# The attention's input product of a two-layer trunk in 24 steps of seven products, with the stored sums of tokens and W_out formed by GpSimd

## What is computed

```python
def _gla_mixer(x, w_in, w_gk, b_gk, norm_w, w_out):
    h = (x @ w_in).astype(jnp.float32)          # (2048, 1024) @ (1024, 3088)
    q, k, v, g, lr = jnp.split(h, [512, 1024, 2048, 3072], axis=-1)
    gk = jax.nn.log_sigmoid(lr @ w_gk + b_gk) / 16
    ...                                          # per head: cumulative sums of gk over chunks of 64,
    qe, ke, kd = q * exp(bcum), k * exp(-bcum), k * exp(b_last - bcum)
    ...                                          # attention of qe, ke, kd, v; norm; times silu(g)
    return o.astype(x.dtype) @ w_out
```

## Time and profile before

| | |
|---|---|
| median of 3 runs | 2005.15 us (2003.45 to 2006.34) |
| profiled execution, own time | 2001.48 us |
| its span, first to last instruction | 1999.6 us |
| TensorE busy | 1914.5 us (96%) |
| VectorE, ScalarE, GpSimd busy | 1161.7, 701.3, 431.5 us |

### The profile page before, as it was taken

The page is one execution under the profiler, slowest core; times in us unless marked ns, Lnnn a source line. Parts: engine busy times, 40 slices in busy tenths (PEclk is TensorE's granted clock), DMA queues, the critical chain, the costliest instruction groups (busy, mean ns, idle before and its releaser), DMA issues.

```text
span 1999.6 us, 24456 instructions
## 1 busy us (share of the span) xinstructions
PE 1914.5 (96%) x8974; PEld 1588.5 (79%) x8974; DVE 1161.7 (58%) x1539; ACT 701.3 (35%) x1065; POOL 431.5 (22%) x268
## 2 busy tenths in 40 slices
PE   8999999999999989999949999999999999999997
PEld 7778887888888778888738888887888886787786
DVE  4330102332415277787675688868678657546998
ACT  4441213131313243343354444344434335224331
POOL 0005200000000000000043666423334343322430
PEclk9999999999999999999979999999999999999999
DMA  8766530334233464455322444333322225647342
GB/s 254 221 202 239 178 103 17 108 87 118 79 101 87 159 242 164 172 187 170 136 96 74 153 141 152 135 104 137 129 88 73 94 74 193 249 170 272 129 177 95
DMA packets 229912, 287.74 MB, mean 144 GB/s; under 512 B 17216, under 2 KB 170176, under 8 KB 227904
## 3 DMA queue, kind: packets, MB, share of 16 engines
q1 hardware_dynamic: 225216, 278.20, 42.0%
q10 hardware_dynamic: 4608, 8.39, 1.1%
HBM read 186.93 MB, written 99.61 MB: 143 GB/s over the span
## 4 chain that ended last, share of the span: by engine, by line
PE 41%; DVE 4%; issue 4%; ACT 1%; POOL 0%; DVEq 0%; POOLq 0%; ACTq 0%
PE banks L165 13%; PE banks L166 13%; PE banks L167 13%; DVE m_w_lo L1922 1%; DVE m_x_lo L1936 1%; ACT m_x_hi L1728 0%; DVE m_x_lo L1914 0%; PE banks L1621 0%; PE banks L1668 0%; DVE m_stats L2025 0%; DVE m_x_lo L1896 0%; DVE m_res L2019 0%; DVE m_res L2035 0%; POOL m_s L1859 0%; DVE m_win_b L1968 0%
## 5 line engine op out<-in xcount | busy, mean ns | idle before, releaser
L165 PE MATMUL banks<-m_x_hi,m_w_hi 128*128 128x512 f32 x1320 | 517.6, 392 | 9.4 <-DVE m_res L2019 3.5
L166 PE MATMUL banks<-m_x_lo,m_w_hi 128*128 128x512 f32 x1320 | 515.3, 390 | 0.0
L167 PE MATMUL banks<-m_x_hi,m_w_lo 128*128 128x512 f32 x1320 | 515.0, 390 | 0.0
L165 PEld LDWEIGHTS banks<-m_x_hi,m_w_hi 128*128 128x128 f32 x1320 | 248.7, 188 | 63.7 <-DVE m_w_lo L1922 10.0
L166 PEld LDWEIGHTS banks<-m_x_lo,m_w_hi 128*128 128x128 f32 x1320 | 248.8, 188 | 52.0 <-issue 0.7
L167 PEld LDWEIGHTS banks<-m_x_hi,m_w_lo 128*128 128x128 f32 x1320 | 248.7, 188 | 52.0
L1854 POOL TENSOR_TENSOR m_s<-pair_raw 128x512 f32<-128x512 f32 x24 | 47.3, 1969 | 891.6 <-POOLq L947 757.5
L165 PE MATMUL banks<-x_hi,h_w_hi 128*128 128x512 f32 x512 | 199.9, 390 | 0.8 <-DVE h_g_out L833 0.8
L166 PE MATMUL banks<-x_lo,h_w_hi 128*128 128x512 f32 x512 | 199.3, 389 | 0.0
L167 PE MATMUL banks<-x_hi,h_w_lo 128*128 128x512 f32 x512 | 199.3, 389 | 0.0
L1716 ACT ACTIVATE m_w_hi<-m_s 128x512 fp32r<-128x512 f32 x184 | 115.5, 629 | 202.7 <-PE banks L167 179.2
(11 more groups left out here) (220 smaller groups left out, 3117.7 us busy)
## 6 DMA issues: line engine op xcount, KB each, us to landing
p_in<-in_pool_w_in SPq DMA_DIRECT2D x32, 256.0 KB, 4.9
p_rows<-in_x SPq DMA_DIRECT2D x16, 512.0 KB, 5.2
w_fused<-p_out SPq DMA_DIRECT2D x32, 256.0 KB, 3.9
h_out_rows<-in_pool_w_out SPq DMA_DIRECT2D x16, 512.0 KB, 6.7
v_tiles<-v_out ACTq DMA_DIRECT2D x32, 256.0 KB, 2.1
w_terms<-h_out_terms SPq DMA_DIRECT2D x8, 1024.0 KB, 5.6
h_raw<-in_gla_w_in SPq DMA_DIRECT2D x16, 512.0 KB, 4.2
g_tiles<-h_g_out SPq DMA_DIRECT2D x32, 256.0 KB, 2.3
```

The lines of the kernel that those rows point to most:

```text
L165: nc.tensor.matmul(out, a_hi, b_hi, start=first, stop=False, skip_group_check=True)
L166: nc.tensor.matmul(out, a_hi, b_lo, start=False, stop=False, skip_group_check=True)
L167: return nc.tensor.matmul(out, a_lo, b_hi, start=False, stop=last, skip_group_check=True)
```

## The change

The input product is cut into 24 steps (`STEPS`), eight for the values (`V_STEPS`, i = 0 to 7: one pair of token tiles by all 1024 value columns) and twice eight for gates, queries and keys (one unit of 2x128 columns by one half of 1024 tokens). A step is seven block products of four `split_product`s each, in the order `ORDER`, position `n` of a step; the names 1 to 7 are block products. One operand (`w_hi[j]`, `w_lo[j]`, 128x512 each) is new in each step: ScalarE rounds it (`hi_part`), VectorE makes the rest (`lo_part`), one step ahead. The other operand (`b_hi[j]`, `b_lo[j]`, 128x2048 each, seven of them) stays for eight steps: first W_v, then either half of x.

- `prepare` no longer splits x. It stores the turned tiles to device memory (`x_in`, 16 stores of 512 KB), loads the four blocks of W_v (1 MB each, SP at n = 10, 12, 14, 16), has GpSimd form their sums (16 operations), and has ScalarE and VectorE split the seven blocks at n = 18, 20, ... 30, ScalarE behind a wait for all 16 sums.
- Each step's pair of blocks (two transfers of 512 KB into `raws[i % 2]`) is loaded by SP; GpSimd forms its four sums (`weight_sums`). In the value steps GpSimd also forms one round of W_out's sums (`out_terms`) and four sums of the tokens (`x_terms`), both into the one buffer `terms`, each stored by SP (1 MB) before the next writes it. The token sums go to `x_in`, from which the seven blocks of a half of x are loaded at steps 7 and 15 (`load_x`, 1 MB each).
- The gate's first factor, cumulative sums, queries, keys and gates are the same arithmetic over halves of 1024 tokens, placed by tables (`Q_AT`, `K1_AT`, ...) in step and position. `load_qkv` stands behind the last stores of the stage. `w_fused` is stored in rows, and read by columns in the last stage.

```diff
 def prepare(nc, p, a):
+    V_LOADS_AT = {10: 1, 12: 7, 14: 3, 16: 2}
+    V_PARTS_AT = {n: j for n, j in zip(range(18, 32, 2), ORDER)}
...
+                def store_x(t):
+                    sp.wait_ge(x_copied, t + 1)
...
                 b11, b12, b22, b21 = (p.b_raw[j] for j in V_LOADS)
+                for j in V_LOADS:
+                    pool.wait_ge(b_loaded[j], DMA)
+                for k in range(HALF_K):
+                    nc.gpsimd.tensor_tensor(p.b_raw[5][:, k, :], b12[:, k, :], b11[:, k, :], ALU.subtract)
...
                     if n >= 1:
                         copy_out(n - 1)
+                    if n in V_PARTS_AT:
+                        act.wait_ge(b_summed, 4 * HALF_K)
+                        j = V_PARTS_AT[n]
+                        nc.scalar.activation(p.b_hi[j][:], p.b_raw[j][:], ACT.Copy).then_inc(b_hi_done, 1)
...
 def project(nc, p, a):
+            def product(i, n):
+                j = ORDER[n]
+                pe.wait_ge(w_lo_done, PRODUCTS * i + n + 1)
+                free(i, j)
+                for k in range(HALF_K):
+                    last = split_product(nc, shaped(i, bank(i, j)), w_hi[j][:, k, :], w_lo[j][:, k, :],
+                                         moving(i, x_hi[j], k), moving(i, x_lo[j], k), opens and k == 0, k == HALF_K - 1)
...
+            (SP, position n of value step i)
+                        if n == 3:
+                            store_out_terms(i)
+                            if i + 1 < 2 * HALF_K:
+                                load_out_rows(i + 1)
+                        elif n == 5:
+                            sp.wait_ge(x_summed, 4 * (i + 1))
+                            sp.wait_ge(w_lo_done, PRODUCTS * (i + 1))
+                            load_pair(i + 2)
+                            store_v(i, 0)
+                            store_x_terms(i)
...
+            (ACT, position n of step i)
+                    elif n == 0:
+                        seed(i)
+                    elif n == 2:
+                        copy_u2(i)
+                    elif n == 3:
+                        copy_p5(i)
+                    for turn in turning(TURN_HI, i, n):
+                        turn_hi(*turn)
+                    if n >= 0:
+                        hi_part(i + 1, n)
...
+            weight_sums(0)
+            for i in range(STEPS):
+                if i + 1 < STEPS:
+                    weight_sums(i + 1)
+                if i < V_STEPS:
+                    for part in range(2):
+                        out_terms(i, part)
+                    for part in range(2):
+                        x_terms(i, part)
```

More of the change, by code:

```diff
@@ L182, in prepare @@
     t_lo = [p.place(f"p_t_lo{s}", [P, GT, P], F32R) for s in range(2)]
-    out = [p.place(f"p_out{s}", [P, GW]) for s in range(2)]
-    rows = [p.place(f"p_rows{s}", [P, D]) for s in range(ROWS)]
+    assert p.at <= SBUF_END
     with ExitStack():
@@ L459, in project @@
[L459 to L470 removed]
+    chunk_end = p.place("h_chunk_end", [P, HALF_CHUNKS])
@@ new lines, in project, with kind, unit, step_of @@
+    w_src = a["gla_w_in"][0].rearrange("(k p) c -> p k c", p=P)
+    N1, N2 = slice(0, BLK), slice(BLK, HALF)
+    MAIN, ALT = 0, 1
+    def kind(i):
+        return "v" if i < V_STEPS else UNITS[i % EPOCH][0]
+    def unit(i):
+        return (i // EPOCH - 1) * HEADS + UNITS[i % EPOCH][1]
+    def step_of(name, m):
+        return (m // HEADS + 1) * EPOCH + STEP_OF[name, m % HEADS]
+    def due(table, i, n):
+        return [(i - r) // EPOCH * HEADS - HEADS + h for h, (r, at) in table.items()
+                if at == n and (i - r) % EPOCH == 0 and 1 <= (i - r) // EPOCH <= 2]
@@ L472, in _, with gates, gate_stores, turns_to @@
+    def gates(m):
+        return g_alt if m % HEADS == 0 else g_main
+    def gate_stores(m, which):
+        return sum((o % HEADS == 0) == (which == ALT) for o in range(m)) * 4 * DMA
+    def turns_to(e, n):
+        return PRODUCTS * (e - 1) + n + 1
+    gk_ps = p.ps[:, 6:8, :].rearrange("p b t -> p (b t)")
+    CHAINED = 5
+    with nc.Block() as block:
         @block.sync
         def _(sp):
-            def load(h, j):
-                sp.dma_start(raw[j % 2][:], w_src[:, :, ds(w_cols(h, j), P)]).then_inc(loaded[j % 2], DMA)
@@ new lines, in gate_rows, with turn_keys @@
+            def gate_rows(m):
+                pe.wait_ge(gk_lo, m + 1)
+                pe.wait_ge(rank_ready, 2 * (m // HEADS + 1))
+                pe.wait_ge(kn_copied, 2 * m)
+                for n in range(2):
+                    nc.tensor.matmul(p.ps[:, 6 + n, :], w_gk[:], rank[:, n * BLK:(n + 1) * BLK], start=True, stop=True
+                                     ).then_inc(gk_mm, 1)
+            def turn_keys(m):
+                pe.wait_ge(k_done, 2 * m + 2)
+                for n in range(2):
+                    for c in range(HALF_K):
+                        t = n * HALF_K + c
+                        last = nc.tensor.transpose(p.ps[:, 6 + n, c * P:(c + 1) * P], sums[:, t * P:(t + 1) * P], p.ident[:])
+                    last.then_inc(turned, 1)
@@ L859, in attend_and_norm @@
+            norm_of(2 * HEADS - 1)
+    for s in held:
+        nc.gpsimd.sem_clear(s)
+        nc.release_semaphore(s)
 def attend_and_norm(nc, p, a):
@@ L960, in load_w @@
                 sp.dma_start(raw[kt % RAW][:], w_src[:, kt, :]).then_inc(raw_loaded[kt % RAW], DMA)
[L962 to L963 removed]
+            for s, n in enumerate((6 * 4, 2 * 4)):
+                sp.wait_ge(p.g_stored[s], n * DMA)
             for kt in range(RAW):
```

1073 lines of the change are left out of this document (665 added, 408 removed).

## The result

The changed kernel takes 2112.2 us (median of four runs, 2110.9 to 2113.9) beside 2004.9 for the kernel before: 1.0545 times as long, 95% interval 1.0531 to 1.0558. It is slower, as forecast, but by 107 us and not by 53.

The account below looks back on a forecast made before the run. TensorE set the pace before; in the value steps GpSimd's chain would. Second stage +21 (61.7 us saving included), first +21, hand-over +11: +53 on 2001.5 gives 2054.5, median 2058 us; range 2022 to 2090.

Parts of the forecast that it names:

- The closed chain: Value steps: GpSimd's sums and their transfers follow without overlap, 28.7 us per round, bounds 25.3 and 32, against TensorE's 19.04.
- product 7 as the place of TensorE's wait: Value steps: TensorE waits once per step at product 7 for `copy_u2`, about 9 us.
- The end of step 8: Second stage: step 8's last product ends near S+253, after the last block of x lands and is split.
- The saved 61.7 us: TensorE's work: 272 fewer matmuls save 61.7 us if nothing else moves.
- The chain costs 81.6 us: Value steps: nine steps end near S+253, where TensorE's pace alone takes 171.4 us; the chain adds 81.6.
- S+30: Value steps: the first token sums end 30 us after S, the second stage's first matmul.
- For stalls I add 8: Second stage after the value steps: VectorE's load, fullest in step 15, stalls TensorE 8 us, bounds 0 and 35.
- The rival of VectorE as the bound: Last 16 steps: VectorE sets the pace, 2 us more in every step, +30, total 2088 us; chance 0.12.
- +21; bounds 10 and 32: First stage: tile 19 waits for W_v's sums, +17, and six other blocks' splits add +4; +21 us.
- T+13.5: Hand-over: third stage starts 13.5 us behind the last matmul T, after copies, stores, issues and landing; +11, bounds 6 and 15.
- Third and last stage at nothing: Third and last stage: no change in length, 0 us in the forecast's sum.
- Contention (2072): Value steps, rival: every pair sum takes 2.0 us, round 30.7 us, +14, total 2072 us; chance 0.15.

Follow-up runs that it names:

- two ways of breaking it: Against the changed kernel: token sums first with W_out's sums formed in place in their own rows, 2032.1 us; or W_out's sums left out, 2029.7 us.
- short pair sums: The changed kernel with GpSimd's pair sums of steps 10 to 23 cut to one column; 2097.4 us, 1.0465 times before.
- W_v loaded earlier: The changed kernel with W_v's four blocks loaded at tiles 2, 4, 6, 8 of the first stage; 2101.1 us, 1.0497 times before.
- all together: The changed kernel with two buffers, third stage's first loads ahead, W_v at tiles 4, 7, 10, 12 and its rest later; 2008.3 us, 1.0031 times before.

## Why the prediction was right and wrong

**Right: direction and mechanisms.** The closed chain (the changed kernel's timeline, and two ways of breaking it, each worth 80 us), product 7 as the place of TensorE's wait, the wait for W_v's sums near tile 19, the landing behind the hand-over: each stands in the profile. The end of step 8 was right by its length alone (24.0 us behind the token sums for 22): the path named was the last block of x, and it was pair 9, ahead of the fifth block's rest in VectorE's stream. The saved 61.7 us of TensorE's work are there too, by the count: the rest of the second stage after the value steps needs 285.6 + 21.8 + 8 = 315.4 us and has 347.2, the value steps need 171.4 and have 269.3, and 616.5 is the sum.

**Wrong: the sizes.** On its own time the profiled execution was forecast at 2054.5 us and took 2111.0. The 56.5 us between are these steps of it:

- *"The chain costs 81.6 us"*: it costs 269.3 - 171.4 = 97.9, 16.3 more. The first token sums begin at 192.16 and end 2.0 us later than S+30. Then come seven rounds, to 400.93, of 29.8 us for 28.7: +7.9. Loads and stores were sized well (6.45 for 6.6, 5.66 for 5.8), and so were the pair sums (6.3 for 6.1); the term that failed is W_out's sums, taken at their undisturbed 5.1 us, which measured 6.4. The token sums of step 7 run beside VectorE's rests of the blocks of x and took 9.7 us instead of 5.1 (last section): +4.5. From there to the end of step 8 is 24.0 us for 22, by another path than the one named.
- *"For stalls I add 8"*: 31.8, 23.8 more, the largest miss and the step that failed most. The prediction took VectorE's load for step 15, let steps of which the sum fits pass for free, and put the lower clock behind a wait at nothing here. Of the 31.8, 21.4 are twelve waits of TensorE, most of them for VectorE's and ScalarE's sums, gates and copies (434.5 to 782 us):

```profile
PE banks L824 <- DVE h_sums L1235: 8.6, 5, 3.7
PE banks L173 <- DVE h_g_main L1131: 5.5, 3, 2.3
PE banks L173 <- ACT h_c L914: 5.3, 2, 2.7
```

  The rest is mostly clock. Around five of the waits, of 1.8 to 3.7 us, the granted clock is 0.50 for 3.4 us each, as here behind the wait of 2.65 us at 479.82 (columns as in the table of stages):

```profile
479.80:482.80 3.00, 2.98 (x7) 2.42 (x8) 2.57 (x5) 0.91 (x2) 0.00 (x0) 0.50 0.08 23
```

  By these figures some 17 us are run at half the pace, an estimated 8 us lost. The short pair sums show 10 of the 32 to be GpSimd's. That the other 22 come from the places of sums, gates and splits in VectorE's and ScalarE's streams was only read, not tried. The rival of VectorE as the bound would have made this term 38 (my 8 and its 30), nearer to 31.8 than 8; in its form, an even 2 us in every step, it is not what the profile shows.
- *"+21; bounds 10 and 32"* for the first stage: +30.0, 9 more, inside the bounds. GpSimd's first sum was taken at 76 and ran at 80.5, which puts tile 19 at +21.5 for +17: 4.5 of it. Behind tile 19 come +8.5 for +4: the six short waits are 6.0 us and not 4, and behind the wait of 14.9 us the clock is 0.50, so that the next twelve matmuls start 0.43 us apart and not 0.23, 2.4 us in all. ScalarE also reached its wait for the sums at 90.5 and not at 83.1, held by a store of `w_fused`; here the sums hid that, in *W_v loaded earlier* it comes out. TensorE's waits for `p_in` are 12.3 us for 8.2 before; the new one (4.8 us) lies ahead of tile 19 while the sums are awaited, and costs nothing further.
- *"T+13.5"* for the hand-over: the third stage begins 17.0 us behind the end of the last product, 17.4 behind its start, from which the forecast counts: 3.9 more. The first store of g is at T+6.4. Its four issues take 2.5 us, the five loads of the first tile 3.1 (priced at 2), and from the last of these issues to TensorE's start it is 5.5 (landing priced at 3 to 4).
- *Third and last stage at nothing*: +3.7. In the profiles of the changed kernel and the nine others these stages, the same in all but one of them, take 1307.3 to 1311.2 us, so up to 4 us of spread is in any single profile. All ten are above the one profile of before (1306.8), so that `w_fused` is now read by columns may have a part in it; this was not tried.

The range ended at 2090 because its ends came from one deviation at a time. Contention (2072) came true in part, though in W_out's sums and not in the pair's, where it was forecast; so did the VectorE case (2088) in size, and the first stage and the hand-over lie near their upper bounds; those summed would have been 2054.5 + 14 + 30 + 11 + 4, beyond 2110.

## What to carry to other kernels

Before moving work to an idle engine, write its round with the transfers that it waits for as a closed chain, and compare that chain, not the engine's busy time, with the pace of the engine that sets the end: one shared buffer between two stores, with the order around it, cost 80 us here, while the same 164 us of GpSimd's work, in a better order and with a buffer for each kind of sum, fitted beside TensorE's. When a cheaper product also moves operand preparation ahead of a stage and stores behind it, the boundaries between stages are part of the price (22 us in the best version, more than the 19 us that the stage gained). Mis-sized terms of one cause (one engine's contention, one fuller queue) go the same way, so a range must add them. A stretch whose sums of work fit still waits where its streams cross, and a longer wait can bring a stretch at the lower clock with it.

## What the hardware showed that was not expected

GpSimd and VectorE slow each other in both directions. VectorE's 128x512 splits, 0.69 us alone, in the value steps (its groups there):

```profile
L1116 DVE TENSOR_TENSOR h_w_lo<-h_s,h_w_hi 128x512 fp32r<-128x512 f32 x39 | 50.2, 1291 | 5.3 <-ACT h_w_hi L847 2.6
```

take 1.29 us. And GpSimd's token sums, 1.29 us each at 222.55 above, beside VectorE's 128x2048 rests (timeline of GpSimd):

```profile
400.93 3.29 POOL L1090 TENSOR_TENSOR h_terms<-h_raw 128x512 f32<-128x512 f32 x1 [7.42 <-DMA w_terms<-h_terms]
...
405.87 3.34 POOL L1094 TENSOR_TENSOR h_terms<-h_raw,h_terms 128x512 f32<-128x512 f32 x1
```

take up to 3.34. The Trainium skill, page "GPSIMD Engine Reference", section "Specifications", says that GpSimd shares its SBUF interfaces with VectorE and contends with VectorE's instructions that have two SBUF inputs, as these splits have. The traces agree, and give the size: up to 2.6 times for GpSimd, 1.9 times for VectorE in the mean of this group.

SP's issues are not free at a stage's end. Its timeline at the hand-over of the changed kernel:

```profile
787.80 2.29 SPq L672 DMA_DIRECT2D g_tiles<-h_g_main  x4
790.33 0.68 SPq L145 DMA_DIRECT2D q<-q_tiles  x1
...
796.07 0.43 SPq L149 DMA_DIRECT2D v<-v_tiles  x1
```

These four stores and ten loads take 8.7 us, 0.43 to 0.69 us each, and all engines meet behind the last of them.

TensorE's granted clock after an idle time. Windows of the changed kernel behind a gap of 7.97 us and behind one of 0.93 us (columns as in the first table of stages):

```profile
206.70:209.70 3.00, 2.99 (x7) 2.43 (x8) 2.85 (x3) 2.12 (x4) 3.00 (x3) 0.50 0.46 185
...
125.10:128.10 3.00, 3.00 (x13) 2.41 (x14) 0.69 (x1) 1.11 (x3) 0.00 (x0) 1.00 0.52 152
```

Behind the long one TensorE runs at 0.50 of full, the lower level of 1.2 GHz, with 7 matmuls in 3 us where 13 run behind the short one at 2.4 GHz. So the short waits of the first stage cost only their own length, other than the expectation of all together had it; five of the longer ones in the second stage's last 15 steps, and the one of 14.9 us, have stretches at the lower level beside them (see the accounts of the stalls and of the first stage). In the value steps the lower level costs nothing further, as far as the round sets the pace: the starts behind the seven waits are 29.0 to 30.1 us apart.
